# Taking each map's row maximum in two parts in the later attention tiles of a decoder layer

## What is computed

```python
def one_block(args):                       # 8 blocks of Q_BLOCK = 128 queries
    i, q_i = args
    s = jnp.einsum('bqhmd,bkhmd->bhmqk', q_i, k) * scale
    causal = key_pos[None, :] <= q_pos[:, None]
    s = jnp.where(causal, s, -jnp.inf)
    p = jax.nn.softmax(s, axis=-1)         # subtracts each row's maximum first
    a = p[:, :, 0] - lam * p[:, :, 1]      # two maps per head
    return jnp.einsum('bhqk,bkhd->bqhd', a, v)
```

## Time and profile before

| | |
|---|---|
| Median of 3 runs | 2013.81 us (2013.05 to 2018.65) |
| The profiled execution | 2014.55 us |
| Its span (first to last instruction) | 2012.8 us, so 1.75 us lie around it |
| TensorE matmul busy | 1949.5 us, 97% of the span |
| VectorE busy | 572.0 us, 28% |
| ScalarE busy | 283.5 us, 14% |
| GpSimd busy | 282.3 us, 14% |
| Attention's later units | about 270 to 353 us from the start |
| Output projection and routing | about 355 to 513 us |
| Experts | from about 513 us on |

### The profile page before, as it was taken

One profiled execution on the slowest core, in us unless ns is written; L12 is line 12 of the kernel. 1 busy time (PEld: TensorE's weight loads), 2 busy tenths in 40 slices (PEclk: granted clock), 3 DMA queues, 4 the chain that ended last, 5 costly groups with the idle time before them and its releaser, 6 DMA issues.

```text
span 2012.8 us, 40313 instructions
## 1 busy us (share of the span) xinstructions
PE 1949.5 (97%) x17569; PEld 1571.6 (78%) x17570; DVE 572.0 (28%) x1108; ACT 283.5 (14%) x457; POOL 282.3 (14%) x481
## 2 busy tenths in 40 slices
PE   8999988998799999999999999999999999999996
PEld 4444455554799798889777999988887888989996
DVE  3115667345113121222211222222222222212214
ACT  2001245111101001100100011111011010101103
POOL 0001234166200000000000010010000000101003
PEclk9999999998899999999999999999999999999998
DMA  4210020412888979998999888899999998888855
GB/s 178 85 42 1 1 94 13 155 64 85 305 275 292 358 274 339 337 327 306 352 339 348 305 303 282 294 358 359 318 338 357 330 344 298 297 285 277 289 167 204
DMA packets 232696, 501.84 MB, mean 249 GB/s; under 512 B 8822, under 2 KB 9487, under 8 KB 232498
## 3 DMA queue, kind: packets, MB, share of 16 engines
q1 hardware_dynamic: 219024, 454.53, 62.8%
q0 software_dynamic: 13424, 44.36, 8.9%
q10 hardware_dynamic: 50, 0.01, 0.0%
HBM read 463.70 MB, written 35.23 MB: 248 GB/s over the span
## 4 chain that ended last, share of the span: by engine, by line
PE 92%; issue 2%; DVE 2%; DMA 2%; ACT 1%; SPq 0%; POOL 0%; ACTq 0%; DVEq 0%; POOLq 0%
PE ps L1742 33%; PE ps L1751 23%; PE ps L1778 12%; PE ps L1515 8%; PE ps L1653 6%; PE ps L1509 3%; PE ps L1765 2%; PE ps L1553 1%; PE ps L1771 1%; DVE soft L1056 1%; ACT hT L782 1%; DMA qk<-x_rows 1%; PE ps L1673 1%; PE ps L1592 0%; DMA w_ring<-in_w_in 0%
## 5 line engine op out<-in xcount | busy, mean ns | idle before, releaser
L1778 PE MATMUL ps<-w_ring,hT 128*128 128x512 f32 x576 | 251.8, 593 | 0.0
L1742 PE MATMUL ps<-hT,qk 128*128 128x136 f32 (+5 forms) x1792 | 234.7, 293 | 10.0 <-issue 10.0
L1742 PEld LDWEIGHTS ps<-hT,qk 128*128 128x128 f32 x1792 | 233.2, 192 | 13.2 <-issue 13.1
L1751 PEld LDWEIGHTS ps<-hT,qk 128*64 128x64 f32 x4608 | 230.2, 137 | 10.9 <-issue 10.3
L1742 PE MATMUL ps<-hT,w_ring 128*128 128x136 f32 (+5 forms) x1792 | 235.6, 292 | 0.6 <-DVE hT L1296 0.4
L1751 PE MATMUL ps<-hT,qk 128*64 128x128 f32 (+3 forms) x4608 | 235.0, 264 | 0.0
L1742 PEld LDWEIGHTS ps<-hT,w_ring 128*128 128x128 f32 x1792 | 230.9, 190 | 2.7 <-issue 1.6
L1778 PEld LDWEIGHTS ps<-w_ring,hT 128*128 128x128 f32 x576 | 107.5, 190 | 126.7 <-issue 126.3
L609 POOL DMA_INDIRECT x_rows<-x,hT x44 | 70.3, 1598 | 761.8 <-ACT x L887 371.3
L1515 PE MATMUL ps<-hT,w_ring 128*128 128x512 f32 x384 | 168.9, 595 | 1.3 <-DMA w_ring<-in_w_in 1.3
L874 ACT ACTIVATE hT<-hT 128x768 f32<-128x768 f32 x64 | 53.8, 841 | 792.3 <-DVE hT L1284 792.3
(11 more groups left out here) (261 smaller groups left out, 1664.6 us busy)
## 6 DMA issues: line engine op xcount, KB each, us to landing
w_ring<-in_w_down SPq DMA_DIRECT2D x64, 2048.0 KB, 9.4
qk<-in_w_gate SPq DMA_DIRECT2D x32, 2048.0 KB, 8.1
qk<-in_w_up SPq DMA_DIRECT2D x32, 2048.0 KB
v<-in_w_gate SPq DMA_DIRECT2D x32, 2048.0 KB, 10.7
u_all<-in_w_up SPq DMA_DIRECT2D x32, 2048.0 KB, 9.5
x<-in_b_down SPq DMA_DIRECT2D x32, 512.0 KB
w_ring<-in_w_in SPq DMA_DIRECT2D x3, 2048.0 KB, 9.3
x<-in_x SPq DMA_DIRECT2D x8, 512.0 KB, 9.9
```

What stands on the lines that cost most here:

```text
L1742: ins = pe.matmul(bank[:, m, 0:n], w[g][:, k, m * P:(m + 1) * P], rhs[:, k, 0:n], start=k == 0, stop=k == KC - 1)
L1751: ins = pe.matmul(bank[part, m, 0:n], w[g][:, k, m * P + part.start:m * P + part.stop], rhs[:, k, 0:n], start=k == 0, stop=k == KC - 1)
L1778: ins = pe.matmul(ps[:, 2 * (g % PAIRS), :], aT[:, k, 0:P], w[g][:, k, :], start=k == 0, stop=k == KC - 1)
```

## The change

For units 16 to 31 the maximum of each map is taken in two parts. TensorE raises `scored` also after the first 512 columns of each map, so a unit raises it four times. VectorE, for each map: waits for the first 512 columns, reduces them into a spare column of `soft` (`bias_low`); waits for the masked scores, reduces columns 512 to n - 1 (128 to 512 of them) into the column that the exponential reads; waits for both of its own results, and takes the smaller of the two negated maxima with a `tensor_tensor` of one column, which raises `biased`. The order is: first map low, high, smaller of the two; then the second map the same. It stands where the two `bias` calls stood, behind `combine`. Units 0 to 15 and the order of all else stay as they are. SP's wait for the last scores counts the added signals.

```diff
+        def scores_of(u):
+
+            return 2 * u + 2 * max(0, u - UNITS_A)
...
-                sp.wait_ge(scored, 2 * len(units))
+                sp.wait_ge(scored, scores_of(len(units)))
...
-                    dve.wait_ge(scored, step + 1)
                     if u < UNITS_A:
+                        dve.wait_ge(scored, step + 1)
                         o.did(dve.tensor_tensor(sc[:, n - P:n], sc[:, n - P:n], mask[:, :], ALU.add))
                         o.need()
-                    dve.reduce_max(soft[:, s4, 0:1], sc[:, 0:n], axis=AX, negate=True).then_inc(biased, 1)
+                        dve.reduce_max(soft[:, s4, 0:1], sc[:, 0:n], axis=AX, negate=True).then_inc(biased, 1)
+                        return
+                    dve.wait_ge(scored, scores_of(u) + 3 + m)
+                    o.did(dve.reduce_max(soft[:, s4, 0:1], sc[:, HALF:n], axis=AX, negate=True))
+                    o.need()
+                    dve.tensor_tensor(soft[:, s4, 0:1], soft[:, s4, 0:1], soft[:, 4 + s4, 0:1], ALU.min).then_inc(biased, 1)
+
+                def bias_low(step):
+
+                    u, m = divmod(step, 2)
+                    dve.wait_ge(scored, scores_of(u) + 1 + m)
+                    o.did(dve.reduce_max(soft[:, 4 + step % 4, 0:1], ps[:, 2 * m, :], axis=AX, negate=True))
...
                     if u + 1 < len(units):
-                        bias(2 * u + 2)
-                        bias(2 * u + 3)
+                        for step in (2 * u + 2, 2 * u + 3):
+                            if u + 1 >= UNITS_A:
+                                bias_low(step)
+                            bias(step)
...
                             ins = pe.matmul(ps[:, 2 * m + c // HALF, 0:w], qkT[part, 0, h, i * P:(i + 1) * P],
                                             qkT[part, 1, h, c:c + w], start=True, stop=u < UNITS_A or c + w < (i + 1) * P)
+                            if u >= UNITS_A and c == 0:
+                                ins.then_inc(scored, 1)
```

## The result

| | before | with the change |
|---|---|---|
| Median of 16 runs each | 2015.51 us (2011.33 to 2018.65) | 2020.82 us (2017.08 to 2023.31) |
| Ratio | | 1.0024, 95% interval 1.0018 to 1.0031 |
| Profiled execution, its span | 2014.55, 2012.8 us | 2021.51, 2019.8 us |

The ratio is 4.8 us (3.6 to 6.2) on a run of 2015.5: slower, by less than the 0.3% that was set as the bound, which the interval just reaches. The medians themselves are 5.3 us apart. The forecast was +4.2 us, "same, on the slow side". Its 2018.0 us lies 2.8 us under the measured 2020.82, and 1.7 of them are the starting point: the median of 3 runs that it counted from was 2013.81, that of 16 runs is 2015.51.

The account below looks back on a forecast made before the run. Bound: a circle of scores or `combine`, maxima and exponentials, from T0 (a unit's second exponential done). 0.35 + 3.5 + 0.16 + 0.9 - 0.45 - 0.3 = +4.2 us on 2013.81 gives 2018.0 us; range 2013.6 to 2022.0.

Parts of the forecast that it names:

- map 0, units 18 to 30: First map's split: 3.7 us of added VectorE steps against 3.35 of idle time and overlap regained, net +0.35 us.
- map 1, units 18 to 30: Second map's reductions and minimum outlast the first exponential, so ScalarE waits 0.23 to 0.29 us a unit: +3.5 us.
- units 16 and 17: Stage start: unit 16 free beside projection matmuls; unit 17's map 0 gains 0.08, map 1 loses more, +0.16 us.
- unit 31: Stage end: `leave` holds the first exponential until 350.32 and the second maximum is in time, so no cost.
- minima blocked by GpSimd: New one-column minima stretched when meeting GpSimd's operations: +0.9 us, taken between nothing and 4.0.
- `combine` of unit 20: `combine` now comes behind GpSimd's last product instead of meeting it, since units 18 and 19 are longer: -0.45 us.
- `combine` of the h = 2 units: `take_out` ends earlier against the second exponential's end, so GpSimd's L528 blocks less of the next `combine`: -0.3 us.
- The cap: Most the early start can gain: VectorE's idle time before the reduction, 4.6 us in 10 waits, 0.23% of the run.
- Rival 1: Each of the 28 minima is blocked by GpSimd: 4.0 us in place of 0.9, total +7.3, 2021.1 us; chance 0.23.
- Rival 2: Later `take_out` lets GpSimd miss `combine` in units 18, 22, 26, 30: total +1.5, 2015.3 us; chance 0.12.
- Rival 3: Short VectorE instructions don't overlap the next: 3.4 us more, total +7.6, 2021.4 us; chance 0.04.
- Faster: Run gets faster, needing more than the 4.6 us of idle time and most of rival 2's relief; chance 0.05.

Follow-up runs that it names:

- the last kernel: Kernel taking the first 512 columns' maximum alone (stage 79.60 us); with GpSimd's norm of a finished query tile also left out, its stage was 73.56 us.
- the third profile: The changed kernel profiled a third time, nothing altered: stage 88.15 us, against 88.34 and 89.30 in its first two profiles.

## Why the prediction was right, point by point

The sum was +4.2 us; the stage gives +3.94, +4.90 and +3.75 (against the first profile of before), and the timed runs +4.8 (3.6 to 6.2). By term, in us, from the first profiles:

| term | predicted | measured |
|---|---|---|
| map 0, units 18 to 30, without what moves `combine` or unit 19's scores | +0.35 | 0.0 |
| map 1, units 18 to 30, without blocks | +3.5 | +3.16 |
| units 16 and 17 | 0 and +0.16 | +0.09 and 0.00 |
| unit 31 | 0 | 0.00 without its block |
| minima blocked by GpSimd | +0.9 | +1.1 (2.0 and 1.1 in the other two) |
| TensorE's clock drop, unit 19 | not in the sum | +0.22 (0.29 and 0 in the other two) |
| `combine` of unit 20 | -0.45 | -0.51 |
| `combine` of the h = 2 units | -0.3 | -0.19 |

The mechanism was right, and the nearness of the sum is in part luck. The two map terms and unit 17 together were 0.85 us too high. The blocked minima, the clock drop, unit 16 and the `combine` terms together came out 0.6 higher than the sum had them, and the clock drop was no part of it at all. The 0.9 for the minima was a choice between two bounds, 0 and 4.0.

*What bounds the stage* was right: a circle from T0 through scores or `combine`, the maxima and the exponentials, into which every added step of VectorE goes. Map 0 alone in two parts is at +0.5 (nothing without its clock drop), map 1 alone at +4.8 (3.0 without a blocked minimum and a clock drop): the finding that the second maximum had been hidden behind the first exponential and loses its cover carries nearly the whole result. The lengths of single units came out as well: the h = 2 units are longer by 0.4 to 0.55 us (0.55 forecast), unit 21 by 0.16 (0.2), unit 28 by -0.08 (next to nothing), and unit 19 by 0.22 beside its clock drop (0.2). The predicted spacings of 1.02, 1.16, 1.29 and 1.42 us came out as 0.99, 1.12, 1.26 and 1.39: 0.03 too long each, because short instructions overlap by 0.09 rather than 0.08 and the reductions were some 10 ns shorter (0.683 and 0.278 us against 0.692 and 0.292 in rows 7). Those three hundredths in 13 units are what both map terms were too high by. Unit 16, put down as free, was not: it became 0.09 us longer, and 0.5 shorter where only the first 512 columns are reduced.

*The cap* held: VectorE's idle time of 4.6 us went down to 1.0, and that is what map 0's split pays itself with. Without the early start the stage is 94.8 us, or 91.4 without that profile's clock drops and blocked minima.

*GpSimd* was the term with the widest bounds, and the mechanism came out as a lock, not as a mean. What counts is what the minimum meets: 30 of 32 minima in the first profile are at or under 0.22 us, two are at 0.80. A short GpSimd operation stretches it too, but by little: the one of 0.22 ends with a sum of 0.25 us (282.31 to 282.56). Rival 1 had priced each of 28 minima alike and asked for 4.0 us; it got at most 2.0. What I had not seen is where the long operation would fall: GpSimd's last product starts 2.8 to 3.5 us after T0 of the h = 3 unit, just where the minima are, in each of the four tiles. I had put unit 31 down as free, and its first minimum was blocked (352.93, 0.80 us), for 0.48 us. The rule of the Trainium skill ("SBUF — State Buffer", SBUF: two separate sides) that such operations exclude each other for their whole length was borne out, by the blocked minima ending with GpSimd's product, and by the minimum with one tensor input, which never waits.

*Rival 2* (GpSimd out of the way of `combine`) didn't come: `combine` of units 18, 22, 26 and 30 became 0.01 us longer and 0.07, 0.11 and 0.02 us shorter. *Rival 3* is refuted by the row at 339.76, which starts 0.60 us after an instruction of 0.69. The Trainium skill ("VectorE: DVE Perf Modes", The DRAIN you can't avoid) says that the next operation waits for the pipe to empty, but that one which isn't held starts earlier; the row agrees with the latter. *Faster* didn't come. Outside the stage nothing that the change does is seen, with the end of the program left open as said above.

## What to carry to other kernels

Starting a reduction early is worth no more than the idle time in front of it, and here another instruction of the same engine (`combine`) used most of that time up; look at what the engine does between the release and the start. Before splitting an operation, ask of each copy whether it is on the path or hidden behind a neighbour: here the first map's split just paid for itself, and the second's, hidden until then with nothing to spare, cost 3.2 us. A one-column operation is not free where it sits in a circle: 0.16 us, 0.04 of waiting on each side, and up to 1.02 if it has two SBUF tensor inputs and meets a long GpSimd operation.

## What the runs showed of the hardware

- GpSimd's hold on VectorE is larger than what the change was about. With GpSimd's norm left out, the last kernel's stage fell by 6.0 us, and `combine` in units 18 to 30 ended 3.7 us earlier in sum than in the kernel before. To move that norm, or to give it operations that don't meet `combine`, is the next thing to try; it was not tried.
- TensorE's granted clock dropped to its lower level for 3.4 us six times in the fourteen profiles, each time within the attention's later units: near 281 us in two of three profiles of the change, in the kernel with map 0 alone and in that without the early start; at 310 with map 1 alone; and at 336 without the early start. It never did so there in four profiles of the kernel before. Busy times (PE, PEld, DVE, ACT, POOL) and the granted clock in the changed kernel, during and before:

```profile
281.30:284.80 3.50, 3.23 (x15) 3.17 (x15) 2.44 (x10) 2.08 (x5) 2.69 (x11) 0.51 1.00 348
270.00:281.30 11.30, 9.66 (x55) 5.43 (x51) 7.92 (x21) 5.37 (x12) 2.15 (x3) 1.00 0.50 170
```

  Unit 18's period of 5.26 us is the same in the third profile, without the drop; the cost comes a unit later, where the slowed products keep TensorE from the next scores: 0.22, 0.29, 0.3 and 0.5 us in unit 19, and in one profile 0.86 more, as the delay put a minimum behind GpSimd's product. Where it met scores that were being waited for it cost 0.9 and 1.4 us. TensorE was busy for 9.66 of the 11.30 us before, and for 9.56 in the third profile, which has no drop; what sets it off these runs don't show. A difference of half a microsecond between two single profiles is worth a look at the granted clock first.
- TensorE's wait before the last 16 transposes came out at 2.3 to 3.1 us or at 4.8 to 5.2, in the same kernel from run to run. A single profile of each kernel can therefore differ by over 2 us at the end of the program (20.05 against 23.16 us in the kernel before).
